# Experts' stage with half-piece weight slots, split tokens and outputs, and low parts shared between VectorE and GpSimd

## The chip, the cores and the metric

The kernel runs on one core of a Trainium2 chip, as one program for a whole stack of layers. The metric is the device time of one execution in microseconds (us); a measurement is the median of several executions.

## What is computed

A block of 256 tokens of width 1024 goes through an even layer, an odd layer with experts, and two further layers. The part that matters here is the experts' stage of the odd layer:

```python
def swiglu(h, w_gate, w_up, w_down):
    return (jax.nn.silu(h @ w_gate) * (h @ w_up)) @ w_down

def moe_swiglu(h, router, w_gate, w_up, w_down):     # h: rms_norm(x, g)
    logits = (t @ router).astype(jnp.float32)        # t: 256 x 1024
    top_v, top_i = lax.top_k(logits, TOP_K)          # 2 of 8
    top_w = jax.nn.softmax(top_v, axis=-1)
    gates = jnp.sum(jax.nn.one_hot(top_i, N_EXPERTS) * top_w[..., None], axis=1)
    for e in range(N_EXPERTS):                       # w_gate[e]: 1024 x 3584, w_down[e]: 3584 x 1024
        out = out + gates[:, e:e + 1] * swiglu(t, w_gate[e], w_up[e], w_down[e])
```

All arrays are float32. The weights of the eight experts are 352 MB, which are read once.

## The kernel before

**Split products.** Every large product is made of three products in fp32r: high by high, low by high, high by low (`split_product`, lines 174 to 176). The high part of a weight piece is a rounding copy on ScalarE (L1671 for the experts, L586 for the FFNs), the low part is raw minus high on VectorE (L1792, L593). A piece has 2048 columns in 128 partitions (1 MB).

**Steps and chunks.** The stage goes through steps `q`, one for each expert, and eight more if an expert has more than 128 tokens. A step has seven chunks of 512 hidden columns. A chunk needs six pieces: two of gate, two of up, two of down. TensorE's order in a chunk is: gate (24 products with 512 moving columns, bank 0), turn of the hidden values of the chunk before (L1591, four transposes), up (24, bank 1), down of the chunk before (24, banks 3 and 4). ScalarE makes silu (L1683), VectorE the product of silu and up (L1798), and the high and low parts of the turned hidden values (L1803, L1805).

**Between steps.** The tokens of the next expert are gathered by products of `xn` with a one-hot matrix (L1567, in f32). ScalarE and VectorE make their high and low parts with the norm's gain (L1659, L1783). The expert's output `y` is copied by both (L1711, L1835), brought back to the token order by products with the transposed one-hot matrix that carries the gate's weight (L1617, f32, the transposes are L1628), and added to the residual on VectorE (L1840). The loop runs in this order on TensorE: up of chunk 0, transposes, chunks 1 to 6, last turn, gather for the next step, last down, first half of the next gate 0, bringing back, second half. It does so in the last step too, for a step whose one-hot matrix is empty.

**Buffers.** Raw weights lie in four slots of 2 MB: slot 0 gate, slot 1 up, slots 2 and 3 down in turn. SP loads a slot again when the low parts of both its halves are made (`r_lo`). The high and low parts have three places each; a place is free when TensorE has used the piece three before (`r_used`, `PE_AHEAD`). The same four slots hold the blocks of the mixers (`load_block`); the blocks 16 to 19 wait for `r_end`, which TensorE raises when the stage is over. SP issues in the order: the FFN's pieces 0 (gate, up, down), these four blocks, the FFN's pieces 1. The mixers' and FFNs' functions are outside the experts' part of the diff. GpSimd has no work in the experts' stage.

The engines wait for semaphores only; there is no planner, the order of each engine is written out by hand.

Of the kernel before, what the change touches and what calls it, by code (L numbers as in the profile page):

```python
# [1411 lines left out]
STEPS = 2 * NE + 1  # L1412


PAIRS = 3 * NC
PE_AHEAD = 3


def moe_pair(kind, c):


    def place_of(c):
        if kind == "down":
            return PAIRS - 1 if isinstance(c, int) and c == NC - 1 else 3 * c + 4
        if isinstance(c, int) and c == 0:
            return 0 if kind == "gate" else 1
        return 3 * c - 1 if kind == "gate" else 3 * c

    first = 2 * place_of(c if isinstance(c, int) else 1) % 3
    return place_of(c), (first, (first + 1) % 3)  # L1430


def moe_done(q, kind, c):

    return 2 * (q * PAIRS + moe_pair(kind, c)[0]) + 2 + PE_AHEAD
# [31 lines left out]
def moe_load(sp, m):  # L1467
# [5 lines left out]
    def free(q, pair):  # L1473

        sp.wait_ge(s["r_lo"], 2 * (q * PAIRS + pair) + 2)

    def gate(e, c):
        sp.dma_start(r.wg, wg[bass.ds(e, 1), :, :, bass.ds(c * FC, FC)].rearrange("e p k f -> p (e k) f")).then_inc(s["r_gin"], 16)

    def up(e, c):  # L1480
        sp.dma_start(r.wu, wu[bass.ds(e, 1), :, :, bass.ds(c * FC, FC)].rearrange("e p k f -> p (e k) f")).then_inc(s["r_uin"], 16)
# [11 lines left out]
    def later(q, e, c, slot):  # L1493
        gate_up(q, e, c)
        free(q, 3 * (c - 2) + 4)
        down(e, c, slot)
# [810 lines left out]
```

## Time and profile before

| | us |
|---|---|
| median of 3 runs | 2805.64 |
| lowest and highest | 2803.16, 2812.22 |
| profiled execution, its own time | 2811.21 |
| span of its profile | 2809.0 |
| experts' stage, from the first L1628 to r_end | 706 to 1748 |

The span runs from the first to the last instruction of the core. Times in the views are counted from the span's start. A record of a matmul is longer than the distance to the next one, because matmuls are pipelined; the pace is the distance between the starts. A matmul in f32 has two records. "PEclk" is the granted clock of TensorE as a share of full speed (2.4 GHz).

### The profile page before, as it was taken

The page shows a single profiled execution, that of the slowest core. Times are in us where ns is not written, and L with a number is a line of the kernel's source. Part 1 is how long each engine was busy: PE and PEld are TensorE (multiplying, and loading weights), DVE is VectorE, ACT ScalarE, POOL GpSimd, SP SyncE. Part 2 cuts the span into 40 slices and gives each one's busy share as a digit, 9 for nine tenths or more (in the row PEclk, how much of TensorE's full clock was granted, in tenths as well). Part 3 has the DMA queues.
Part 4 walks back from the last instruction along what each step waited for, and adds up shares of the span by engine and source line. Part 5 has one row for each costly group of instructions (what it writes and reads, how often), then busy time and mean ns, then how long its engine had stood idle before and what let it go on. Part 6 is the DMA issues. An engine that isn't in the chain of part 4 may idle for free.

```text
span 2809.0 us, 36049 instructions
## 1 busy us (share of the span) xinstructions
PE 2583.0 (92%) x14026; PEld 2188.3 (78%) x14026; DVE 1768.8 (63%) x1738; ACT 1258.9 (45%) x1092; POOL 59.6 (2%) x35
## 2 busy tenths in 40 slices
PE   8699997677999999999999999899889999996999
PEld 6499884664778787878787877799659989974898
DVE  4455444443888898989898887455635555555545
ACT  2433301222666676767666766333033343321333
POOL 0000001210000000000000000000100000001000
PEclk9899998887999999999999999999889999998999
DMA  8265142002989898989899999753405575522453
GB/s 311 93 199 179 60 150 90 1 1 90 342 316 358 309 370 299 372 305 375 299 342 336 347 336 332 248 188 105 150 31 186 192 258 179 182 88 75 154 190 127
DMA packets 313325, 601.41 MB, mean 214 GB/s; under 512 B 6064, under 2 KB 130096, under 8 KB 313008
## 3 DMA queue, kind: packets, MB, share of 16 engines
q1 hardware_dynamic: 313264, 600.55, 60.4%
q8 instruction: 43, 0.70, 0.1%
q14 instruction: 18, 0.15, 0.0%
HBM read 599.48 MB, written 1.05 MB: 214 GB/s over the span
## 4 chain that ended last, share of the span: by engine, by line
PE 66%; DVE 7%; DVEq 2%; DMA 2%; ACT 2%; issue 1%; PEld 1%; PEldq 0%; ACTq 0%; SPq 0%
PE bank L174 19%; PE bank L175 18%; PE bank L176 18%; PE bank L445 3%; PE bank L1887 2%; DVE weights_lo L1792 2%; DVE scratch L2026 2%; PE bank L1567 1%; DVEq L2027 1%; PE bank L1591 1%; PE bank L1617 1%; DMA mslot<-in_o_moe_w_up 1%; DMA scratch<-in_ffn_w_gate 1%; DVEq L1778 0%; PE bank L1117 0%
## 5 line engine op out<-in xcount | busy, mean ns | idle before, releaser
L1792 DVE TENSOR_TENSOR weights_lo<-mslot,weights_hi 128x2048 fp32r<-128x2048 f32 x338 | 769.7, 2289 | 86.8 <-ACT weights_hi L1671 82.0
L1671 ACT ACTIVATE weights_hi<-mslot 128x2048 fp32r<-128x2048 f32 x338 | 646.0, 1917 | 254.1 <-PE bank L176 189.1
L593 DVE TENSOR_TENSOR weights_lo<-scratch,weights_hi 128x2048 fp32r<-128x2048 f32 x165 | 377.1, 2292 | 374.8 <-ACT weights_hi L586 372.0
L174 PE MATMUL bank<-x_hi,weights_hi 128*128 128x256 f32 x1760 | 504.4, 287 | 19.3 <-DVE weights_lo L593 10.3
L175 PE MATMUL bank<-x_lo,weights_hi 128*128 128x256 f32 x1760 | 503.6, 286 | 0.0
L176 PE MATMUL bank<-x_hi,weights_lo 128*128 128x256 f32 x1760 | 503.3, 286 | 0.0
L586 ACT ACTIVATE weights_hi<-scratch 128x2048 fp32r<-128x2048 f32 x165 | 315.6, 1919 | 323.0 <-PE bank L176 276.6
L174 PE MATMUL bank<-weights_hi,x_hi 128*128 128x512 f32 x944 | 385.6, 408 | 33.3 <-DVE weights_lo L1792 33.3
L175 PE MATMUL bank<-weights_lo,x_hi 128*128 128x512 f32 x944 | 374.3, 396 | 0.0
L176 PE MATMUL bank<-weights_hi,x_lo 128*128 128x512 f32 x944 | 374.2, 396 | 0.0
L174 PEld LDWEIGHTS bank<-x_hi,weights_hi 128*128 128x128 f32 x1760 | 343.6, 195 | 22.6 <-DVE weights_lo L593 17.6
L175 PEld LDWEIGHTS bank<-x_lo,weights_hi 128*128 128x128 f32 x1760 | 343.7, 195 | 1.7
L176 PEld LDWEIGHTS bank<-x_hi,weights_lo 128*128 128x128 f32 x1760 | 343.5, 195 | 0.0
L174 PE MATMUL bank<-weights_hi,hidden_hi 128*128 128x512 f32 x848 | 331.3, 391 | 0.0
L175 PE MATMUL bank<-weights_lo,hidden_hi 128*128 128x512 f32 x848 | 330.5, 390 | 0.0
L176 PE MATMUL bank<-weights_hi,hidden_lo 128*128 128x512 f32 x848 | 330.0, 389 | 0.0
L174 PEld LDWEIGHTS bank<-weights_hi,x_hi 128*128 128x128 f32 x944 | 181.1, 192 | 80.8 <-DVE weights_lo L1792 36.4
L176 PEld LDWEIGHTS bank<-weights_hi,x_lo 128*128 128x128 f32 x944 | 181.0, 192 | 39.9
L175 PEld LDWEIGHTS bank<-weights_lo,x_hi 128*128 128x128 f32 x944 | 181.4, 192 | 38.0 <-issue 1.9
L176 PEld LDWEIGHTS bank<-weights_hi,hidden_lo 128*128 128x128 f32 x848 | 159.2, 188 | 33.6
L174 PEld LDWEIGHTS bank<-weights_hi,hidden_hi 128*128 128x128 f32 x848 | 159.4, 188 | 31.6 <-DVE weights_lo L1792 0.2
L175 PEld LDWEIGHTS bank<-weights_lo,hidden_hi 128*128 128x128 f32 x848 | 159.4, 188 | 30.9
(346 smaller groups left out, 2312.9 us busy)
## 6 DMA issues: line engine op xcount, KB each, us to landing
mslot<-in_o_moe_w_down SPq DMA_DIRECT2D x58, 2048.0 KB, 8.1
mslot<-in_o_moe_w_gate SPq DMA_DIRECT2D x57, 2048.0 KB, 8.5
...
```

The lines of the kernel that those rows point to most:

```text
L174: pe.matmul(out, stationary[0], moving[0], start=start, stop=False)
L175: pe.matmul(out, stationary[0], moving[1], start=False, stop=False)
L176: return pe.matmul(out, stationary[1], moving[0], start=False, stop=stop)
L445: last = pe.matmul(m.ps[4 + 2 * t + half][:, :], yT[:, k, t * P:(t + 1) * P], mblock(m, i + half)[:, k, :], start=(k == 0), stop=(k == KT ...
L586: act.activation(m.whi[ffn_place(kind, u)][:, :], m.fslot[i], ACT.Copy).then_inc(m.sig["f_hi"], 1)
L593: dve.tensor_tensor(m.wlo[to][:, :], m.fslot[i], m.whi[to][:, :], ALU.subtract).then_inc(m.sig["f_lo"], 1)
L1567: last = pe.matmul(m.ps[k // 4][:, (k % 4) * P:(k % 4 + 1) * P], m.xn[:, t, k * P:(k + 1) * P], r.oh[:, t, :], start=(t == 0), stop=(t == ...
L1591: last = pe.transpose(m.ps[2][:, j * P:(j + 1) * P], r.h[:, j * P:(j + 1) * P], c["ident"])
L1671: act.activation(m.whi[places[half]][:, :], raw[:, half * PIECE:(half + 1) * PIECE], ACT.Copy).then_inc(s["r_hi"], 1)
L1792: dve.tensor_tensor(m.wlo[places[half]][:, :], raw[:, half * PIECE:(half + 1) * PIECE], m.whi[places[half]][:, :], ALU.subtract).then_inc( ...
L1887: last = pe.matmul(m.ps[bank + a // 2][:, (a % 2) * SEQ:(a % 2 + 1) * SEQ], mblock(m, base + j)[:, k, a * P:(a + 1) * P], m.xT[:, k, :], s ...
L2026: eng.scalar_tensor_tensor(c.acc[:, a, :], x, w[:, a, i:i + 1], c.acc[:, a, :], ALU.mult, ALU.add)
```

## The change

- The raw weights lie in six slots of 1 MB (three memories of 2 MB). Each half of a piece is loaded, waited for and freed by itself; a slot is loaded again when both low parts of its last content, VectorE's and GpSimd's, are made (`r_lo`, `r_lp`). The fourth memory lies over xn's high part and other tensors and isn't used in the stage.
- The pieces follow TensorE's order strictly: gate 0, up 0, gate 1, up 1, down 0, gate 2 and so on. Gate 1 of a step is loaded with gate 0 and up 0.
- VectorE makes columns 0 to 1535 of each low part, GpSimd columns 1536 to 2047 (`moe_pool`). TensorE waits for both.
- The tokens are split once: GpSimd multiplies `xn` by the gain, ScalarE makes `xnh`, GpSimd `xnl`. The gather is 16 products of each with the one-hot matrix in fp32r, and ScalarE copies the two results to `xgh` and `xgl`.
- The output is split: `yh` on ScalarE, `yl` on VectorE; bringing back is eight fp32r products with a one-hot matrix without weights, and the gate's weight is applied in the addition.
- The turned hidden values' high part goes from VectorE to ScalarE. VectorE makes the hidden product of a chunk behind the next chunk's gate low parts.
- Bringing back is in two halves, before and after up of chunk 0, and the one-hot transposes follow chunk 1.
- The last step is written out: no gather, no gate of a further step, no loads for one. The first FFN's pieces gate 0 and up 0 are split within the stage.

The diff, added lines of its core (what they replace is printed above):

```diff
-    m.mslot = [sb(f"mslot{i}", KT * HALF) for i in range(4)]
+    m.mslot = [sb(f"mslot{i}", KT * HALF) for i in range(3)]
     m.res = cut(sb("res", NT * D), 0, NT, D)
-    m.xn = cut(sb("xn", NT * D), 0, NT, D)
-    m.xT = cut(sb("xT", KT * SEQ), 0, KT, SEQ)
...
+    with nc.sbuf_tensor("mslot3", [P, KT * HALF], F32) as mslot3, nc.sbuf_tensor("xn", [P, NT * D], F32) as xn, \
+            nc.sbuf_tensor("xT", [P, KT * SEQ], F32) as xT:
+        m.mslot.append(mslot3)
+        m.xn, m.xT = cut(xn, 0, NT, D), cut(xT, 0, KT, SEQ)
+    sb("mslot3_rest", KT * HALF - NT * D)
+    m.xnh, m.xnl = cut(sb("xn_hi", NT * D, F32R), 0, NT, D), cut(sb("xn_lo", NT * D, F32R), 0, NT, D)
+    sb("xT_rest", KT * SEQ - 2 * SEQ)
+    m.oh, m.ohT = sb("one_hot", SEQ, F32R)[:, :], sb("one_hot_T", SEQ, F32R)[:, :]
...
+PIECES = 6 * NC
+PLACES, SLOTS = 3, 6
+PE_AHEAD = PLACES
+POOL_FROM = 1536
+def moe_piece(kind, c):
+    if kind == "gate":
+        return (0, 0, 0, 0) if isinstance(c, int) and c == 0 else (6 * c - 2, 1, 4, c - 1)
+    if kind == "up":
+        return (2, 2, 2, 0) if isinstance(c, int) and c == 0 else (6 * c, 0, 0, c)
+    return (40, 1, 4, 6) if isinstance(c, int) and c == NC - 1 else (6 * c + 8, 2, 2, c + 1)
+def moe_used(q, kind, c):
+    return q * PIECES + moe_piece(kind, c)[0] + 2 + PE_AHEAD
...
+    r.yh, r.yl = (flat(t)[:, KT * P:KT * SEQ] for t in (m.xh, m.xl))
+    xT = flat(m.xT)
+    r.silu, r.h = xT[:, 0:FC], xT[:, FC:2 * FC]
+    r.oh = m.oh.rearrange("p (t s) -> p t s", t=NT)
+    r.oh32, r.ohT = r.oh.bitcast(F32), m.ohT
     r.hh, r.hl = (t[:, :].rearrange("p (j t) -> p j t", j=FC // P) for t in (m.hh, m.hl))
-    r.wg, r.wu = (m.mslot[i].rearrange("p (k n) -> p k n", k=KT) for i in range(2))
-    r.wd = [m.mslot[2 + i].rearrange("p (k n) -> p k n", k=FC // P) for i in range(2)]
+    r.slot = [m.mslot[i // 2][:, i % 2 * PIECE:(i % 2 + 1) * PIECE] for i in range(SLOTS)]
+    r.gain = m.fslot[0][:, 0:D]
...
+    def piece(q, e, kind, c, begin=False):
+        number, _, slot, _ = moe_piece(kind, c)
+        n = D if kind == "down" else FC
+        raw = [half_of(kind, e, c, half) for half in range(2)]
+        if not begin:
+            for part in raw:
+                sp.lower_val(part.offset * 4)
+        for half in range(2):
+            if begin:
+                block_used(sp, m, B_SECOND - 4 + (slot + half) // 2)
+            else:
+                sp.wait_ge(s["r_lo"], q * PIECES + number + half - SLOTS + 1)
+                sp.wait_ge(s["r_lp"], q * PIECES + number + half - SLOTS + 1)
+            sp.dma_start(r.slot[slot + half].rearrange("p (k n) -> p k n", n=n),
+                         raw[half]).then_inc(s[f"r_in{slot + half}"], 16)
     def rest(q, e):
+        piece(q, e, "up", 1)
+        piece(q, e, "down", 0)
+        with sp.Fori(2, NC) as c:
+            piece(q, e, "gate", c)
+            piece(q, e, "up", c)
+            piece(q, e, "down", c - 1)
+        piece(q, e, "down", NC - 1)
+    def first(q, e, begin=False):
+        piece(q, e, "gate", 0, begin)
+        piece(q, e, "up", 0, begin)
+        piece(q, e, "gate", 1, begin)
+    sp.wait_ge(s["d_ota"], 2)
+    sp.wait_ge(s["d_otd"], 2)
+    sp.dma_start(r.gain, w["ln_ffn"][1:2, :].to_broadcast([P, D])).then_inc(s["r_gain"], 16)
+    first(0, 0, begin=True)
+    final = moe_last(sp, m)
+    with sp.Fori(0, final) as q:
+        e, after = sp.snap(q & (NE - 1), min_val=0, max_val=NE - 1), sp.snap((q + 1) & (NE - 1), min_val=0, max_val=NE - 1)
+        rest(q, e)
+        first(q + 1, after)
+    rest(final, NE - 1)
...
     def gather(n):
         pe.wait_ge(s["r_oh"], n + 1)
-                last = pe.matmul(m.ps[k // 4][:, (k % 4) * P:(k % 4 + 1) * P], m.xn[:, t, k * P:(k + 1) * P],
+        for src, banks in ((r.xnh, (5, 6)), (r.xnl, (7, 1))):
+            for k in range(KT):
+                for t in range(NT):
+                    last = pe.matmul(m.ps[banks[k // 4]][:, (k % 4) * P:(k % 4 + 1) * P],
+                                     src[:, t, k * P:(k + 1) * P], r.oh[:, t, :], start=(t == 0), stop=(t == NT - 1))
+            last.then_inc(s["r_gath"], 1)
...
+    def halves(q, kind, ch, k):
+        number, place, _, _ = moe_piece(kind, ch)
+        for half in range(2):
+            pe.wait_ge(s["r_lo"], q * PIECES + number + half + 1)
+            pe.wait_ge(s["r_lp"], q * PIECES + number + half + 1)
+            i = (place + half) % PLACES
+            yield half, [t[i][:, :].rearrange("p (k n) -> p k n", k=k) for t in (m.whi, m.wlo)]
...
     def chunk(q, ch, first=False):
         pe.wait_ge(s["r_silu"], q * NC + ch)
         inner(q, 0, "gate", ch)
+        if first:
+            pe.wait_ge(s["r_add"], q + 1)
         turn(q * NC + ch - 1)
         inner(q, 1, "up", ch)
         down(q, ch - 1, first=first)
+    def begin(q):
+        pe.wait_ge(s["r_xg"], 2 * q + 2)
+        inner(q, 0, "gate", 0)
+    def bring_back(q, t):
+        if t == 0:
+            pe.wait_ge(s["r_ohT"], q + 1)
+            pe.wait_ge(s["r_yl"], 2 * q + 2)
+        for half in range(2):
+            bank, cols = m.ps[((5, 6), (7, 2))[t][half]], slice(half * HALF, (half + 1) * HALF)
+            pe.matmul(bank[:, :], r.ohT[:, t * P:(t + 1) * P], r.yh[:, cols], start=True, stop=False)
+            pe.matmul(bank[:, :], r.ohT[:, t * P:(t + 1) * P], r.yl[:, cols], start=False,
+                      stop=True).then_inc(s["r_scat"], 1)
+    def middle(q, gather_next):
+        chunk(q, 1, first=True)
         for t in range(NT):
+            last = pe.transpose(m.ps[7][:, t * P:(t + 1) * P], r.oh32[:, t, :], c["ident"])
+        last.then_inc(s["r_ohTp"], 1)
         with pe.Fori(2, NC) as ch:
             chunk(q, ch)
         pe.wait_ge(s["r_silu"], q * NC + NC)
         turn(q * NC + NC - 1)
+        if gather_next:
+            pe.wait_ge(s["r_ohT"], q + 1)
+            gather(q + 1)
         down(q, NC - 1, final=True)
+    pe.wait_ge(s["r_xnh"], 1)
+    pe.wait_ge(s["r_xnl"], 1)
+    gather(0)
+    begin(0)
+    inner(0, 1, "up", 0)
+    final = moe_last(pe, m)
+    with pe.Fori(0, final) as q:
+        middle(q, True)
+        begin(q + 1)
+        bring_back(q, 0)
+        inner(q + 1, 1, "up", 0)
+        bring_back(q, 1)
+    middle(final, False)
+    bring_back(final, 0)
+    bring_back(final, 1)
...
+    def hi(q, kind, c, halves=(0, 1)):
+        number, place, slot, filled = moe_piece(kind, c)
+        for half in halves:
+            act.wait_ge(s[f"r_in{slot + half}"], (q * NC + filled + 1) * 16)
+            act.wait_ge(s["r_used"], q * PIECES + number + half + 1)
+            act.activation(m.whi[(place + half) % PLACES][:, :], r.slot[slot + half], ACT.Copy).then_inc(s["r_hi"], 1)
+    def gathered(n):
+        for i, (out, banks) in enumerate(((r.xgh, (5, 6)), (r.xgl, (7, 1)))):
+            act.wait_ge(s["r_gath"], 2 * n + i + 1)
+            for g in range(2):
+                last = act.activation(out[:, 4 * g:4 * g + 4, :], heads4(m.ps[banks[g]]), ACT.Copy)
+            last.then_inc(s["r_xg"], 1)
...
+    def chunk(q, c):
+        hi(q, "gate", c)
+        hi(q, "up", c)
+        hi(q, "down", c - 1, halves=(0,))
+        hidden_hi(q * NC + c - 1)
+        silu(q, c)
+        hi(q, "down", c - 1, halves=(1,))
+    def y_hi(q):
+        act.wait_ge(s["r_used"], moe_used(q, "down", NC - 1))
+        for side in range(2):
+            act.activation(r.yh[:, side * HALF:(side + 1) * HALF], m.ps[3 + side][:, :],
+                           ACT.Copy).then_inc(s["r_yh"], 1)
...
+    hi(0, "gate", 0)
+    act.wait_ge(s["r_xn"], 1)
+    act.activation(r.xnh, m.xn, ACT.Copy).then_inc(s["r_xnh"], 1)
     act.wait_ge(s["r_e"], 1)
     act.activation(r.ex, r.ex, ACT.Exp).then_inc(s["r_ed"], 1)
-        hi(q, "gate", c, m.mslot[0], "r_gin", q * NC + c + 1, halves)
-        hi(q, "up", c, m.mslot[1], "r_uin", q * NC + c + 1)
-        hi(q, "down", c - 1, m.mslot[2 + slot], f"r_din{slot}", chunks)
+    hi(0, "up", 0, halves=(0,))
...
+        middle(q)
+        hi(q + 1, "gate", 0, halves=(0,))
         gathered(q + 1)
+        hi(q + 1, "gate", 0, halves=(1,))
+        y_hi(q)
+        hi(q + 1, "up", 0)
+        silu(q + 1, 0)
+    middle(final)
+    act.wait_ge(s["r_used"], moe_used(final, "down", NC - 2))
+    ffn_hi(act, m, 1, "gate", 0)
+    y_hi(final)
+    ffn_hi(act, m, 1, "up", 0)
...
+def moe_pool(pool, m):
+    s, r = m.sig, moe_mem(m)
+    pool.wait_ge(s["r_gain"], 16)
+    pool.wait_ge(s["n_tr"], 4 * 3 + 4)
+    pool.tensor_tensor(m.xn, m.xn, bc(r.gain, 1, NT), ALU.mult).then_inc(s["r_xn"], 1)
+    pool.wait_ge(s["r_xnh"], 1)
+    pool.tensor_tensor(r.xnl, m.xn, r.xnh, ALU.subtract).then_inc(s["r_xnl"], 1)
+    def lo(q, kind, ch):
+        number, place, slot, _ = moe_piece(kind, ch)
+        for half in range(2):
+            pool.wait_ge(s["r_hi"], q * PIECES + number + half + 1)
+            i, cols = (place + half) % PLACES, slice(POOL_FROM, PIECE)
+            pool.tensor_tensor(m.wlo[i][:, cols], r.slot[slot + half][:, cols], m.whi[i][:, cols],
+                               ALU.subtract).then_inc(s["r_lp"], 1)
+    def rest(q):
+        with pool.Fori(1, NC) as ch:
+            lo(q, "gate", ch)
+            lo(q, "up", ch)
+            lo(q, "down", ch - 1)
+        lo(q, "down", NC - 1)
+    lo(0, "gate", 0)
+    lo(0, "up", 0)
+    final = moe_last(pool, m)
+    with pool.Fori(0, final) as q:
+        rest(q)
+        lo(q + 1, "gate", 0)
+        lo(q + 1, "up", 0)
+    rest(final)
...
+    def lo(q, kind, ch, halves=(0, 1)):
+        number, place, slot, _ = moe_piece(kind, ch)
+        for half in halves:
+            dve.wait_ge(s["r_hi"], q * PIECES + number + half + 1)
+            i, cols = (place + half) % PLACES, slice(0, POOL_FROM)
+            dve.tensor_tensor(m.wlo[i][:, cols], r.slot[slot + half][:, cols], m.whi[i][:, cols],
+                              ALU.subtract).then_inc(s["r_lo"], 1)
...
+    def chunk(q, ch, last=False):
+        hidden(q, ch - 1)
+        lo(q, "up", ch)
+        lo(q, "down", ch - 1, halves=(0,))
+        hidden_lo(q * NC + ch - 1)
+        lo(q, "down", ch - 1, halves=(1,))
+        if not last:
+            lo(q, "gate", ch + 1)
+    def y_lo(q):
+        for side in range(2):
+            cols = slice(side * HALF, (side + 1) * HALF)
+            dve.wait_ge(s["r_yh"], 2 * q + side + 1)
+            dve.tensor_tensor(r.yl[:, cols], m.ps[3 + side][:, :], r.yh[:, cols], ALU.subtract).then_inc(s["r_yl"], 1)
+    def add(q, t, half):
+        dve.wait_ge(s["r_scat"], 4 * q + 2 * t + half + 1)
+        x = m.res[:, t, half * HALF:(half + 1) * HALF]
+        return dve.scalar_tensor_tensor(x, m.ps[((5, 6), (7, 2))[t][half]][:, :], r.gates[:, t, bass.ds(q, 1)], x,
+                                        ALU.mult, ALU.add)
...
+    with dve.Fori(0, final) as q:
+        middle(q, True)
+        lo(q + 1, "gate", 0)
+        y_lo(q)
+        lo(q + 1, "up", 0)
+        add(q, 0, 0)
+        add(q, 0, 1)
+        lo(q + 1, "gate", 1)
+        add(q, 1, 1)
+        add(q, 1, 0).then_inc(s["r_add"], 1)
+    middle(final, False)
+    ffn_lo(dve, m, 1, "gate", 0)
+    y_lo(final)
+    add(final, 0, 0)
+    add(final, 0, 1).then_inc(s["n_res"], 1)
+    add(final, 1, 0).then_inc(s["n_res"], 1)
+    add(final, 1, 1).then_inc(s["n_res"], 1)
+    norm_scale(dve, m, AFTER_EXPERTS, 0)
+    ffn_lo(dve, m, 1, "up", 0)
...
```

## Rows read from the trace of the kernel before

**Rows 1.** Windows: span, busy (count) of PE, PEld, DVE, ACT, POOL, PEclk, DMA share, GB/s.
```profile
733.00:817.00 84.00, 84.00 (x397) 69.89 (x396) 77.62 (x50) 59.26 (x41) 0.00 (x0) 1.00 0.96 352
...
835.32:967.23 131.91, 128.61 (x575) 104.53 (x574) 114.40 (x80) 89.17 (x62) 0.00 (x0) 0.97 0.91 334
967.23:1098.01 130.78, 127.48 (x576) 103.60 (x575) 114.37 (x80) 90.98 (x62) 0.00 (x0) 0.99 0.92 337
...
1623.94:1729.80 105.86, 102.11 (x459) 83.40 (x458) 96.58 (x61) 72.17 (x43) 0.00 (x0) 1.00 0.96 350
```

**Rows 2.** Chain that ended last, 700 to 1000 us: start, us, what.
```profile
782.90 0.44 PE bank L1591 x4
...
799.71 0.44 PE bank L1591 x4
...
811.52 3.57 PE bank L1567 x32
...
823.28 3.45 PE bank L1617 x8
...
839.36 0.43 PE bank L175
```

**Rows 3.** Timeline of TensorE behind a step's border; idle time before in brackets.
```profile
838.56 0.80 PE L174 MATMUL bank<-weights_hi,x_hi 128*128 128x512 f32 x1 [2.86 <-DVE weights_lo L1792]
```

**Rows 4.** Timeline of ScalarE and VectorE at the same border.
```profile
829.49 0.60 ACT L1683 ACTIVATE xT<-bank 128x512 f32<-128x512 f32 x1 [1.96 <-PE bank L176]
832.74 3.71 ACT L1671 ACTIVATE weights_hi<-mslot 128x2048 fp32r<-128x2048 f32 x2 [2.65 <-DMA mslot<-in_o_moe_w_gate]
...
835.62 0.69 DVE L1798 TENSOR_TENSOR xT<-xT,bank 128x512 f32<-128x512 f32 x1 [3.77 <-PE bank L176]
```

**Rows 5.** Tail: ScalarE's and TensorE's timeline, and a window of saturated DMA.
```profile
1748.40 1.28 ACT L360 ACT_TABLE_LOAD   x1 [8.32 <-PEq L1645]
...
1777.99 3.71 ACT L586 ACTIVATE weights_hi<-scratch 128x2048 fp32r<-128x2048 f32 x2 [11.13 <-DMA scratch<-in_ffn_w_gate]
...
1782.28 0.58 PE L174 MATMUL bank<-x_hi,weights_hi 128*128 128x256 f32 x1 [10.29 <-DVE weights_lo L593]
...
1747.00:1777.00 30.00, 18.18 (x118) 16.82 (x116) 9.20 (x14) 13.56 (x23) 0.00 (x0) 0.88 1.06 373
```

**Rows 6.** Groups and single lines: duration by shape on VectorE and GpSimd.
```profile
L1792 DVE TENSOR_TENSOR weights_lo<-mslot,weights_hi 128x2048 fp32r<-128x2048 f32 x338 | 769.7, 2289 | 86.8 <-ACT weights_hi L1671 82.0
...
L1396 DVE TENSOR_TENSOR xn<-xn,small x2: 1209/1214/1218, 590.0 to 623.8; 128x1024 f32<-128x1024 f32 x2
...
L1178 POOL TENSOR_TENSOR scratch<-scratch,consts x12: 2342/2354/3323, 474.3 to 587.7; 128x1024 f32<-128x1024 f32 x12
...
L2070 POOL TENSOR_TENSOR scratch<-scratch 128x768 f32<-128x768 f32 x4 | 7.2, 1799 | 0.6
```

**Rows 7.** Timeline of VectorE and GpSimd, 472 to 482 us, another stage.
```profile
475.99 1.72 DVE L1353 TENSOR_TENSOR scratch<-scratch,consts 128x1024 f32<-128x1024 f32 x1
477.78 3.20 DVE L1355 TENSOR_TENSOR scratch<-consts,scratch 128x1024 f32<-128x1024 f32 x1
...
474.28 5.63 POOL L1178 TENSOR_TENSOR scratch<-scratch,consts 128x1024 f32<-128x1024 f32 x2 [7.83 <-DVE scratch L1348]
```

**Rows 8.** Timeline of TensorE in an FFN: 256 moving columns, fp32r.
```profile
1829.82 0.28 PE L174 MATMUL bank<-x_hi,weights_hi 128*128 128x256 f32 x1
1829.94 0.28 PE L175 MATMUL bank<-x_lo,weights_hi 128*128 128x256 f32 x1
```

**Rows 9.** Timeline of TensorE from the first gather to chunk 1 of step 0.
```profile
680.82 5.40 PE L1567 MATMUL bank<-scratch,xn 128*128 128x128 f32 x32 [3.45 <-DVEq L1778]
...
692.70 0.77 PE L174 MATMUL bank<-weights_hi,x_hi 128*128 128x512 f32 x1 [6.48 <-DVE weights_lo L1792]
...
709.31 0.50 PE L174 MATMUL bank<-weights_hi,x_hi 128*128 128x512 f32 x1 [2.86 <-DVE weights_lo L1792]
```

More of the change, by code:

```diff
@@ L1402, in odd_norm_dve @@
     dve.tensor_tensor(x, x, bc(o.v["orr"][:, th], 2, P), ALU.mult).then_inc(s["d_on"], 1)
[L1412 to L1435, printed above, removed]
+STEPS = 2 * NE
+PIECES = 6 * NC
[10 more added lines that the diff above has]
+    return q * PIECES + moe_piece(kind, c)[0] + 2 + PE_AHEAD
 def moe_mem(m):
@@ L1471, in moe_load @@
     wd = w["o_moe_w_down"][0].rearrange("e (k p) n -> e p k n", p=P)
[L1473 to L1481, printed above, removed]
-    def down(e, c, slot):
-        sp.dma_start(r.wd[slot], wd[bass.ds(e, 1), :, bass.ds(c * (FC // P), FC // P), :]
-                     .rearrange("e p k n -> p (e k) n")).then_inc(s[f"r_din{slot}"], 16)
@@ L1487, in gate_up @@
-    def gate_up(q, e, c):
-        free(q, 3 * (c - 1) - 1 if not isinstance(c, int) or c > 1 else 0)
-        gate(e, c)
-        free(q, 3 * (c - 1) if not isinstance(c, int) or c > 1 else 1)
-        up(e, c)
[L1493 to L1496, printed above, removed]
-    def rest(q, e):
-        gate_up(q, e, 1)
-        with sp.Fori(1, 3) as j:
-            later(q, e, 2 * j, 0)
-            later(q, e, 2 * j + 1, 1)
-        later(q, e, NC - 1, 0)
@@ L1594, in down @@
     def down(q, ch, first=False, final=False):
[L1595 to L1596 removed]
+        pe.wait_ge(s["r_hl"], q * NC + ch + 1)
+        for half, (hi, lo) in halves(q, "down", ch, FC // P // 2):
             for j in range(FC // P // 2):
@@ new lines, in y_hi, with middle @@
+    def y_hi(q):
[3 more added lines that the diff above has]
+                           ACT.Copy).then_inc(s["r_yh"], 1)
+    def middle(q):
+        chunk(q, 1)
+        act.wait_ge(s["r_ohTp"], q + 1)
+        act.activation(r.ohT, m.ps[7][:, 0:SEQ], ACT.Copy).then_inc(s["r_ohT"], 1)
+        with act.Fori(2, NC) as c:
+            chunk(q, c)
+        hi(q, "down", NC - 1)
+        hidden_hi(q * NC + NC - 1)
@@ L1732, in first_best, with one_hot, hidden, hidden_lo @@
         dve.drain()
+    def lo(q, kind, ch, halves=(0, 1)):
[5 more added lines that the diff above has]
+                              ALU.subtract).then_inc(s["r_lo"], 1)
+    def one_hot(n):
+        for t in range(NT):
+            dve.tensor_scalar(r.oh[:, t, :], c["iota"], r.rank[:, t, bass.ds(n, 1)], None, ALU.is_equal)
+        dve.drain().then_inc(s["r_oh"], 1)
+    def hidden(q, ch):
+        dve.wait_ge(s["r_used"], moe_used(q, "up", ch))
+        dve.wait_ge(s["r_silu"], q * NC + ch + 1)
+        dve.tensor_tensor(r.h, r.silu, m.ps[1][:, :], ALU.mult).then_inc(s["r_h"], 1)
+    def hidden_lo(i):
+        dve.wait_ge(s["r_hh"], i + 1)
+        dve.tensor_tensor(r.hl, heads4(m.ps[2]), r.hh, ALU.subtract).then_inc(s["r_hl"], 1)
+    def chunk(q, ch, last=False):
[16 more added lines that the diff above has]
+                                        ALU.mult, ALU.add)
+    def middle(q, more):
+        chunk(q, 1)
+        chunk(q, 2)
+        if more:
+            dve.wait_ge(s["r_ohTp"], q + 1)
+            one_hot(q + 1)
+        with dve.Fori(3, NC - 1) as ch:
+            chunk(q, ch)
+        chunk(q, NC - 1, last=True)
+        hidden(q, NC - 1)
+        lo(q, "down", NC - 1)
+        hidden_lo(q * NC + NC - 1)
     first_best(r.lg, r.m1, r.sel1)
```

251 lines of the change are left out of this document (51 added, 200 removed).

## The prediction

> **What bounds the kernel now.** I read the windows of whole expert steps first, then the chain and the timeline inside one chunk and at one step's border, then the tail. The page's busy shares are averages over stages; what counts is what ends last in the experts' stage. It has eight steps, one per expert (no overflow round). I measure a step from one pair of L1628 transposes to the next: 131.91 and 130.78 us alternate, mean 131.35 [rows 1]. From the first gate product of chunk 1 in step 0 (709.31) to the last turn of the hidden values (1729.80) it takes 1020.5 us [rows 1, 9].
>
> Inside a step TensorE paces the chunks: from turn to turn 799.71 - 782.90 = 16.81 us; less 0.44 for the turn that is 0.227 for each of 72 products, with no wait between [rows 2]. VectorE follows closely, 77.6 of 84 us busy, and DMA has a share of 0.96 at 352 GB/s [rows 1].
>
> Outside its seven chunks (117.6) a step costs 13.7 us: gather L1567 3.57, bringing back L1617 3.45 [rows 2], the two transposes some 0.25, and 6.4 more. Of this 2.9 are a hole before gate piece 1 of chunk 1 [rows 3], and most of the rest is clock: behind the hole, up to which TensorE had run nearly without a gap, the products come every 0.43 us instead of 0.227, half of full speed, so 1.2 GHz, for about 3 us of loss in one step and 1 in the next (granted clock 0.97 and 0.99 over the step) [rows 1, 2]. The hole has an order behind it: ScalarE has made that piece's high part (from 832.74, 1.9 us), but VectorE has the hidden product of chunk 0 first, which waits for the up products until 835.62; then come 0.69 of its own and 2.29 for the low part [rows 4].
>
> **Tail.** After the last turn the kernel gathers and multiplies for a ninth step that nothing uses: gather 3.6, down 5.45, half a gate 2.7, bringing back 3.45, the other half 2.7; r_end comes at 1748.40. SP loads 8 MB for it as well. Then come FFN loads (3.1 MB), four mixer blocks (6.8 MB) and only then FFN gate piece 1, copied at 1777.99; TensorE, idle for 10.3 us, restarts at 1782.28 [rows 5]. DMA is saturated there, 373 GB/s over 30 us [rows 5]: the ceiling I use.
>
> **The change, part by part.**
>
> *Steady chunk.* The 72 products and the turn stay: 16.8. What must hold is the loop of a piece: products of piece n-3 done, high part, low part, products of piece n. TensorE gives it two pieces, 5.45 us. The high part takes 1.9 [rows 4]; for the hand-over from TensorE I allow 0.2, for the others 0.05 each.
>
> The low part is now 1536 columns on VectorE and 512 on GpSimd, both released by the high part. VectorE takes 2.289 us for 2048 columns and 1.214 for 1024: 1.05 ns a column, 1.75 us for 1536, 1.60 without the start. GpSimd takes 1.80 for 768 and 2.354 for 1024: 2.16 ns a column, 1.25 us for 512, 1.11 without the start [rows 6]. Do they overlap? One place of the trace answers. GpSimd starts two L1178 at 474.28; VectorE's L1353 and L1355, with two SBUF inputs each, start at 475.99 and 477.78 and take 1.72 and 3.20 where the same size takes 1.21 alone [rows 6, 7]. Laid out with 2.34 for GpSimd's first: it ends at 476.62, VectorE's at 477.71 (1.09 later), GpSimd's second at 479.91 (2.20 later), VectorE's at 480.98 (1.07 later). They take turns by whole instructions, only the starts are hidden. So a low part lasts 1.60 + 1.11 = 2.71 and 0.15 for the start, against 2.29 now: GpSimd's help makes it later by 0.5. Six take 16.3 of a chunk's 16.8. The loop is 0.2 + 1.92 + 0.05 + 2.86 + 0.05 = 5.1 against 5.45, so the chunk stays at 16.8 with 0.35 in hand. The hidden product and hidden_lo (0.69 each) read one operand from PSUM; I take it that GpSimd goes ahead beside them. Bounds of a piece on this port: 2.25 (VectorE as now; no gain, TensorE sets 2.80) and 1.75 + 1.25 = 3.0. ScalarE takes hidden_hi (0.60) over and has 12.7 of 16.8.
>
> The Trainium skill states this for the shared port (SBUF — State Buffer, Who interferes with whom): a VectorE instruction with two SBUF inputs and a GpSimd one that reads SBUF exclude each other for their whole length. By that rule, the trace agrees with 1.72 and 3.20 against 1.21. Were the two side by side instead, a piece would be ready after 1.75 and the loop would have 1.4 in hand: the same sum, and rival D would fall away.
>
> *DMA.* Six slots of 1 MB instead of four of 2 MB; SP now waits for both engines' low parts. A slot is free when its low parts are made and needed six pieces later, less the three in the works: 12 us, room for four pieces on the way. A step's 44.04 MB at 373 GB/s are 118 us, less than the step below: hidden, as are SP's 42 issues. Without that cover each 0.1 us a piece costs 4 us a step.
>
> *Gather.* 32 fp32r products of 128 columns instead of 16 in f32, whose two records make 0.223 us each. No row has fp32r at 128 columns. Lower bound: 0.12 at 256 columns [rows 8] and 0.227 at 512 give 0.42 ns a column and 0.013, so 0.067 each, 2.1 in all. Between: a record as now, 0.11, 3.6. Upper: 0.223 each, 7.1. Nearest in shape is L1567 itself; I take 7.1 and keep 2.1 for the range. ScalarE's four copies lie beside the down products.
>
> *Border.* Bringing back is 8 fp32r products, 1.8 instead of 3.45. Gate piece 1 lies in its slots before the step and is split ahead of the hidden product, so the hole goes, and with it the low clock. y is copied (two of 0.60) and y_lo made (two of 0.69) beside gate 0. The tightest is the first up half: high part from +1.3 to +3.2 after down's end, low part to +6.05; TensorE wants it at 5.45 + 0.9 = 6.35. If a piece slips there, 1 to 2 us a step come back.
>
> New step: 117.6 + 0.25 + 7.1 + 1.8 = 126.8. The last, from gate 1 to its last turn, is 0.25 + 6 x 16.81 = 101.1. Together 7 x 126.8 + 101.1 = 988.7 against 1020.5: 31.8 less.
>
> *Start.* GpSimd multiplies xn by the gain (2048 columns, about 4.4 us) while the router works. ScalarE can't split gate 0 before r_used (677.3), then copies xn_hi until 683.1; xn_lo ends at 687.7. Gather at the slow pace of the first one now (5.40 instead of 3.57) takes 8.9 and the copies 1.4: products begin at 698.0 instead of 692.70, but gate 1 waits for nothing: 708.9 against 709.31 [rows 9]. 0.4 less.
>
> *Tail.* From the last turn: 0.45, down 5.45, y_hi and y_lo 2.2, bringing back 1.8, drain: r_end at +10.2 instead of +18.6. The blocks start there, with 3.1 MB fewer ahead of gate piece 1: 8.4 us at 373 GB/s. TensorE restarts at +10.2 + (33.9 - 8.4) = +35.7 instead of +52.5: 16.8 less. The FFN pieces made early, and the norm, lie before that restart and cost nothing while gate piece 1 sets it. The shared memory of mslot3 with xn_hi is covered by the same r_end.
>
> Sum: 31.8 + 0.4 + 16.8 = 49.0. The profiled execution took 2811.2 (span 2809.0), so 2762.2. The median of the runs is 5.6 lower: 2757.
>
> **The rivals.**
>
> A, the forecast: 2757, its own range 2745 to 2775.
>
> B, the gather costs 3.6 or less. For: one record of it takes 0.11 now. Against: f32 at 128 columns costs four times the stream. 28 us less, 2729; at 2.1 us 2717.
>
> C, small waits stay at the border (the first up half) or 0.05 us a piece in the chunks: 2 to 4 us a step, 2773 to 2790.
>
> D, the other sign: the shared port becomes the bound. Place: the low parts in the chunks. If GpSimd and all of VectorE's chunk go strictly in turns, six times 3.0 and 0.69 twice make 19.4, 2.6 over TensorE. With one piece regained during the gather a step is 126.8 + 7 x 2.6 - 2.8 = 142, eight make 123 us: 2880. It eats the gain from 49/8 = 6.1 a step on: (6.1 + 2.8)/42 = 0.21 over 2.80, so from 3.01 us a piece. For: 2.71 is only 0.09 under the pace. Against: the turns above hide their starts, and the hidden products read PSUM.
>
> That the new slots do nothing, as DMA is the bound anyway, would take 44.04 MB/126.8 = 347 GB/s as ceiling; the 373 speaks against it.
>
> **How the numbers follow.** A 0.42, B 0.27, C 0.14, D 0.17 (0.05 of it within 0.3%). The range, 2714 to 2806, holds A, B, C and D's mild end, and leaves some 0.17 out. A measurement here tells about 0.3% (8 us) from no change. Faster 0.79, same 0.05, slower 0.16.
>
> **What would show it.** Steps 127 us apart; gather records 0.22 apart (B: 0.07 to 0.11); turns 16.8 apart inside a step, VectorE's 1536 columns at 1.75 or up to 2.9 behind GpSimd; no hole and no lower clock behind the border; restart 36 us after the last turn. Wrong, towards D, if turns inside a step are over 17.3 us apart and TensorE waits for low parts there.

## The result, and the profile after the change

| | before | after |
|---|---|---|
| median of 4 runs, us | 2808.30 | 2824.19 |
| lowest and highest | 2803.16, 2812.22 | 2823.81, 2824.57 |
| profiled execution, its own time | 2811.21 | 2824.29 |
| span of its profile | 2809.0 | 2822.5 |

The ratio is 1.006 (95% interval 1.0045 to 1.0075): slower by 0.6%, where 2757 was forecast. The chip's profile says where it went. First the windows, of two whole steps and of three stretches in the second, around the transposes (columns as in [rows 1]):

```profile
861.21:994.51 133.30, 126.52 (x576) 103.90 (x575) 100.91 (x64) 90.53 (x63) 105.64 (x42) 0.97 0.92 330
994.51:1127.80 133.29, 126.53 (x576) 103.90 (x575) 100.87 (x64) 90.48 (x63) 105.53 (x42) 0.97 0.92 330
...
985.00:993.00 8.00, 7.84 (x35) 6.21 (x34) 6.03 (x4) 2.75 (x3) 2.80 (x2) 1.00 1.03 373
993.00:1002.00 9.00, 3.60 (x14) 2.78 (x13) 4.71 (x3) 5.89 (x4) 4.71 (x2) 0.76 0.32 114
...
1000.20:1004.30 4.10, 4.02 (x10) 3.19 (x11) 4.10 (x3) 0.62 (x1) 4.10 (x2) 0.50 0.67 219
```

A step takes 133.3 us; it took 131.35 [rows 1], and 126.8 was forecast. From gate 1 of step 0 to the last turn it takes 1041.8 us instead of 1020.5. TensorE is busy for 3.6 of the 9 us behind 993, and behind that its granted clock is 0.50. Its timeline: two turns of the hidden values, the transposes and what follows them, and the gather.

```profile
874.65 0.60 PE L1587 MATMUL bank<-consts,xT 128*128 128x128 f32 x4
...
891.44 0.60 PE L1587 MATMUL bank<-consts,xT 128*128 128x128 f32 x4
...
994.50 0.38 PE L1629 MATMUL bank<-consts,one_hot 128*128 128x128 f32 x2
1000.28 0.77 PE L182 MATMUL bank<-weights_hi,x_hi 128*128 128x512 f32 x1 [5.40 <-POOL weights_lo L1747]
1000.84 0.63 PE L183 MATMUL bank<-weights_lo,x_hi 128*128 128x512 f32 x1
1001.27 0.63 PE L184 MATMUL bank<-weights_hi,x_lo 128*128 128x512 f32 x1
...
1088.66 1.98 PE L1563 MATMUL bank<-one_hot,xn_hi 128*128 128x128 f32 x16
1090.48 1.95 PE L1563 MATMUL bank<-one_hot,xn_lo 128*128 128x128 f32 x16
1092.27 0.44 PE L182 MATMUL bank<-weights_hi,hidden_hi 128*128 128x512 f32 x1
```

Turns inside a step stay 16.79 apart (16.81 before, [rows 2]), but for one pair in each of the seven steps with a next one: there (891.44 to 910.08 in this step) it is 18.64, with waits of 0.63 for a low part and 0.59 for hidden_lo in chunk 3. That was the prediction's sign towards rival D, and it shows in one chunk of seven. The old hole behind the border [rows 3] is gone, and so is the low clock behind it. A new one of 5.40 us stands right behind the transposes, ahead of gate of chunk 2, in all eight steps, and behind it the products come 0.43 apart, at 1.2 GHz, until 1004.3. The releaser named is GpSimd's low part, but an engine that is named last is not yet the cause. One goes back along the same stretch on ScalarE, VectorE and GpSimd:

```profile
994.91 0.38 ACT L1703 ACTIVATE one_hot_T<-bank 128x256 fp32r<-128x256 f32 x1 [6.87 <-PE bank L1629]
995.31 5.51 ACT L1668 ACTIVATE weights_hi<-mslot 128x2048 fp32r<-128x2048 f32 x3
...
997.25 4.50 DVE L1791 TENSOR_TENSOR weights_lo<-mslot,weights_hi 128x1536 fp32r<-128x1536 f32 x2 [6.22 <-ACT weights_hi L1668]
...
997.29 8.38 POOL L1747 TENSOR_TENSOR weights_lo<-mslot,weights_hi 128x512 fp32r<-128x512 f32 x3 [7.88 <-ACT weights_hi L1668]
```

ScalarE had been idle for 6.87 us, waiting for the transposes, with its copy of them (L1703). Behind the copy in its order stand the high parts of gate of chunk 2, whose raw weights had long been loaded; three of them then come in one burst. VectorE and GpSimd were idle for 6.22 and 7.88 us behind it. TensorE, which runs the transposes at the end of chunk 1, finds all three places empty: copy 0.4, high part 1.9, low part 3.0, together with the hand-overs 5.4.

The low parts of the experts over the whole stage (duration in ns: least, median, most), and the one-hot matrix on VectorE:

```profile
L1791 DVE TENSOR_TENSOR weights_lo<-mslot,weights_hi x336: 1746/1866/2860, 679.0 to 1751.7; 128x1536 fp32r<-128x1536 f32 x168
L1747 POOL TENSOR_TENSOR weights_lo<-mslot,weights_hi x336: 1263/2812/2878, 688.6 to 1751.9; 128x512 fp32r<-128x512 f32 x168
...
L1796 DVE TENSOR_SCALAR one_hot<-consts,tiny x16: 281/1324/1343, 681.4 to 1554.3; 128x128 fp32r<-128x128 f32 x16
```

At the start, answering to [rows 9], and at the end, answering to [rows 5] (TensorE, ScalarE, SP's issues, and two windows behind r_end):

```profile
688.70 3.64 PE L1563 MATMUL bank<-one_hot,xn_hi 128*128 128x128 f32 x16 [11.74 <-POOL xn_lo L1740]
...
696.93 0.79 PE L182 MATMUL bank<-weights_hi,x_hi 128*128 128x512 f32 x1 [1.17 <-ACT x_lo L1674]
...
710.51 0.47 PE L182 MATMUL bank<-weights_hi,x_hi 128*128 128x512 f32 x1 [0.62 <-POOL weights_lo L1747]
...
1752.31 0.60 PE L1587 MATMUL bank<-consts,xT 128*128 128x128 f32 x4
1754.50 0.47 PE L182 MATMUL bank<-weights_hi,hidden_hi 128*128 128x512 f32 x1 [1.59 <-DVE hidden_lo L1806]
...
1762.24 0.75 PE L1622 MATMUL bank<-x_hi,one_hot_T 128*128 128x512 f32 x1 [2.01 <-DVE x_lo L1821]
1762.78 0.63 PE L1623 MATMUL bank<-x_lo,one_hot_T 128*128 128x512 f32 x1
1763.21 0.63 PE L1622 MATMUL bank<-x_hi,one_hot_T 128*128 128x512 f32 x1
...
1794.37 0.58 PE L182 MATMUL bank<-x_hi,weights_hi 128*128 128x256 f32 x1 [8.43 <-DVE weights_lo L601]
...
1790.08 5.51 ACT L594 ACTIVATE weights_hi<-scratch 128x2048 fp32r<-128x2048 f32 x3 [9.26 <-DMA scratch<-in_ffn_w_gate]
...
1766.05 7.42 SPq L225 DMA_DIRECT2D mslot<-in_w_in  x4
...
1766.00:1772.00 6.00, 2.52 (x15) 2.28 (x16) 4.31 (x7) 3.67 (x12) 0.00 (x0) 0.76 0.84 273
1766.05:1790.08 24.03, 16.20 (x112) 15.39 (x112) 7.49 (x14) 7.83 (x20) 0.00 (x0) 0.85 1.01 348
```

From the last turn to the FFN's restart it takes 42.1 us (52.5 before). The steps eat that gain of 10.4 and more: they lose 21.3.

### The profile page after: what moved, and what is told of

It reads as the page before. It is cut to its first block, busy times and chain, and to the rows that moved or that the text cites. A ratio compares the mean times of both kernels' runs of the same rounds, so it can differ in the third digit from the quotient of the medians.

```text
span 2822.5 us, 37757 instructions
## 1 busy us (share of the span) xinstructions
PE 2568.6 (91%) x13970; PEld 2184.4 (77%) x13970; DVE 1653.0 (59%) x1592; ACT 1264.7 (45%) x1100; POOL 921.7 (33%) x373
## 4 chain that ended last, share of the span: by engine, by line
PE 37%; POOL 22%; issue 13%; DVE 4%; DVEq 1%; ACT 1%; DMA 1%; POOLq 1%; SPq 0%; PEldq 0%; ACTq 0%; PEld 0%
POOL weights_lo L1747 22%; PE bank L182 10%; PE bank L183 10%; PE bank L184 10%; PE bank L453 3%; PE bank L1945 2%; DVE scratch L2084 2%; DVEq L2085 1%; DMA scratch<-in_ffn_w_gate 1%; PE bank L1125 0%; PE bank L1124 0%; POOLq L1751 0%; PE bank L1116 0%; SPq L225 0%; PE bank L429 0%
## 5 line engine op out<-in xcount | busy, mean ns | idle before, releaser
L1747 POOL TENSOR_TENSOR weights_lo<-mslot,weights_hi 128x512 fp32r<-128x512 f32 x336 | 851.8, 2558 | 214.4 <-ACT weights_hi L1668 212.8
L1791 DVE TENSOR_TENSOR weights_lo<-mslot,weights_hi 128x1536 fp32r<-128x1536 f32 x336 | 685.7, 2051 | 271.7 <-ACT weights_hi L1668 270.6
L182 PE MATMUL bank<-weights_hi,x_hi 128*128 128x512 f32 x936 | 378.1, 404 | 49.3 <-POOL weights_lo L1747 43.8
```

The lines of the kernel that those rows point to most:

```text
L182: pe.matmul(out, stationary[0], moving[0], start=start, stop=False)
L1747: pool.tensor_tensor(m.wlo[i][:, cols], r.slot[slot + half][:, cols], m.whi[i][:, cols], ALU.subtract).then_inc(s["r_lp"], 1)
L1791: dve.tensor_tensor(m.wlo[i][:, cols], r.slot[slot + half][:, cols], m.whi[i][:, cols], ALU.subtract).then_inc(s["r_lo"], 1)
```

## The experiments

The first theory (T) was the one above: the copy's place in ScalarE's order. Its rival (P) was the shared port: the hole is released by GpSimd, and GpSimd's low parts take 2.81 us at the median. The first four kernels form a table of the two, with one alone on the kernel before. All are compared with the kernel before on the same chip; its medians there were 2808.1 (first four kernels), 2806.4 and 2806.2, so times of different series compare to some 2 us.

**Copy of the transposes one place later.** ScalarE makes the high parts of gate of chunk 2 first.

```diff
         chunk(q, 1)
+        hi(q, "gate", 2)
         act.wait_ge(s["r_ohTp"], q + 1)
         act.activation(r.ohT, m.ps[7][:, 0:SEQ], ACT.Copy).then_inc(s["r_ohT"], 1)
-        with act.Fori(2, NC) as c:
+        hi(q, "up", 2)
+        ...
+        with act.Fori(3, NC) as c:
             chunk(q, c)
```

> The changed kernel with one move in ScalarE's order: the copy of the transposed one-hot matrix stands behind the two high parts of gate in chunk 2 instead of ahead of them. Order theory (the hole of 5.4 us behind chunk 1 comes from ScalarE waiting for the transposes with three empty places behind it, and the low clock from the hole): the hole falls under 0.7 us, the granted clock of a step rises from 0.97 to over 0.99, a step goes from 133.2 to 123.5 to 125 us, the time to about 2824 - 8 x 9 = 2752 (2740 to 2765). Port theory (GpSimd's low parts are what is late): the hole moves or shrinks by under 1 us, time 2815 to 2825.

Measured: 2763.24, ratio 0.9837 (0.982 to 0.9853): 61.0 below the changed kernel, 7.6 for each of eight steps. A step, and the two waits of TensorE over 0.3 us that are left in each step, both in chunk 3 (here of the next step):

```profile
853.66:979.28 125.62, 124.30 (x575) 102.37 (x574) 101.03 (x65) 90.64 (x63) 103.96 (x43) 1.00 0.97 351
...
1002.98 0.50 PE L182 MATMUL bank<-weights_hi,x_hi 128*128 128x512 f32 x1 [0.54 <-DVE weights_lo L1797]
1009.37 0.47 PE L182 MATMUL bank<-weights_hi,hidden_hi 128*128 128x512 f32 x1 [0.60 <-DVE hidden_lo L1812]
```

The hole is gone and the granted clock stays at 1.00. Theory T holds for the hole. The time lies in its range (2740 to 2765), the step (125.6) just above its own (123.5 to 125): something is left. One place in one engine's order decides between slower and faster than before.

**All low parts on VectorE** (`POOL_FROM = PIECE`, `moe_pool` without its low parts, no waits for `r_lp`), first on the changed kernel, then with the copy later.

> The changed kernel with all 2048 columns of each low part on VectorE; GpSimd only multiplies by the gain and makes xn_lo. Order theory: the hole behind chunk 1 shrinks only by the low part's difference (2.8 to 2.3), from 5.4 to 4.9 us, a step is 131 to 133 us, time 2805 to 2822. Port theory: the hole goes, step 124, time about 2750.

> Both edits: the copy behind gate of chunk 2, and all low parts on VectorE. Order theory: about as the first kernel, as low parts are hidden in either: 2745 to 2760; faster than the first by up to 5 us if the waits of 0.6 in chunk 2 come from the port. Were VectorE (2.25 x 6 + 2 x 0.69 = 14.9 of 16.8 a chunk) too busy at the border, slower than the first by up to 8 us.

Measured: 2800.04, ratio 0.997 (0.9958 to 0.9983), for the first, with a hole of 4.72 in every step; that is 5 us below theory T's range, and far from the 2750 of theory P. And 2745.57, ratio 0.9777 (0.976 to 0.9794), for both. A step of it:

```profile
848.09:971.33 123.24, 123.24 (x576) 102.59 (x575) 108.05 (x65) 90.71 (x63) 0.00 (x0) 1.00 0.98 357
```

TensorE is busy for 123.24 of 123.24 us: 117.6 for the chunks, 3.57 for the gather, 1.82 for bringing back, 0.25 for the transposes. The kernel is 17.7 faster than with the copy alone, where at most 5 were expected. So the hole doesn't need GpSimd (the last low part ahead of it only takes 2.29 instead of 2.81), and GpSimd's quarter costs 2.4 us a step that theory T doesn't hold. Where the hole stands, it costs more: 24.2 us between the changed kernel and the first of these two, and the copy is then worth 54.5. The two don't simply add: the shorter low part also shortens the hole, 4.72 instead of 5.40.

**GpSimd's quarter alone, on the kernel before** (`lo` on VectorE up to column 1536, the rest on GpSimd, TensorE and SP wait for both).

> The kernel before with one part of the change alone: GpSimd makes columns 1536 to 2047 of each low part. Each low part then lasts 2.8 instead of 2.3 us. Order theory (the port costs little): the hole before gate 1 grows by 0.5 us, a step by 0.5 to 1.5: 2810 to 2820. Port theory: chunks go from 16.8 to 17.5 or more, time over 2840.

Measured: 2814.64, ratio 1.0021 (1.0012 to 1.0031); steps of 129.9 to 133.7, mean 131.7, about as expected. It is 0.2% slower: in the old order too the help doesn't help.

**Half of each low part on GpSimd** (copy later, `POOL_FROM = 1024`): do the engines take turns, or does GpSimd slow down beside VectorE?

> The first kernel of the first series (copy behind gate of chunk 2) with GpSimd's share of each low part doubled: columns 1024 to 2047. Turns theory (VectorE and GpSimd exclude each other on the shared port): a piece takes 1.07 + 2.2 = 3.27 us of it, over TensorE's 2.80, so a chunk takes 19.4 to 19.8 instead of 16.8 and the time is 2763 + 8 x 13 to 8 x 17 = 2867 to 2900. If they ran side by side, GpSimd's 2.35 would stay hidden and the time would be 2755 to 2765.

Measured: 2908.45, ratio 1.0354 (1.0328 to 1.038). Consecutive waits of TensorE in a chunk, and GpSimd's low parts:

```profile
1076.69 0.47 PE L182 MATMUL bank<-weights_hi,hidden_hi 128*128 128x512 f32 x1 [0.34 <-POOL weights_lo L1753]
1080.04 0.47 PE L182 MATMUL bank<-weights_hi,x_hi 128*128 128x512 f32 x1 [0.38 <-POOL weights_lo L1753]
1083.39 0.47 PE L182 MATMUL bank<-weights_hi,x_hi 128*128 128x512 f32 x1 [0.38 <-POOL weights_lo L1753]
...
L1753 POOL TENSOR_TENSOR weights_lo<-mslot,weights_hi x336: 2346/3383/3455, 688.1 to 1839.4; 128x1024 fp32r<-128x1024 f32 x168
```

And VectorE's and GpSimd's low parts beside each other, 20 us earlier:

```profile
1056.34 1.23 DVE L1797 TENSOR_TENSOR weights_lo<-mslot,weights_hi 128x1024 fp32r<-128x1024 f32 x1 [2.15 <-ACT weights_hi L1668]
1059.06 1.85 DVE L1797 TENSOR_TENSOR weights_lo<-mslot,weights_hi 128x1024 fp32r<-128x1024 f32 x1 [1.49 <-ACT weights_hi L1668]
...
1056.42 6.76 POOL L1753 TENSOR_TENSOR weights_lo<-mslot,weights_hi 128x1024 fp32r<-128x1024 f32 x2
```

The first of GpSimd's two ends at 1059.83 by the trace, 2.26 behind VectorE's first part (1057.57), and VectorE's second part ends 1.09 behind that (1060.92). These are turns by whole instructions; neither engine works slower beside the other (alone, 2.35 and 1.21 with their starts).

A piece every 3.35 us is the sum of both engines' parts less their starts (1.21 + 2.35 = 3.56 with them, [rows 6]; 3.27 was expected, and the time lies 8 us above the range). This is the mechanism of rival D, seen at the share at which it becomes the bound.

**An eighth on GpSimd, and no one-hot matrix for the next steps** (both with the copy later). What are the 2.4 us a step that GpSimd's quarter costs? The first kernel sets `POOL_FROM = 1792`. The second leaves out the next steps' one-hot matrices (two 128x128 compares become two single columns), so all steps use the first expert's tokens.

> The first kernel of the first series with GpSimd's share halved: columns 1792 to 2047. If VectorE and GpSimd take turns, a piece holds the port for 1.87 + 0.55 = 2.42 us instead of 2.71, and what waits for GpSimd waits 0.7 instead of 1.25: step 123.3 to 124.7, time 2746 to 2757. If the loss doesn't depend on the share: 2760 to 2764.

> The first kernel of the first series (copy behind gate of chunk 2, GpSimd's quarter kept) without the 128-column one-hot instructions of the following steps: two instructions of one column take their place, so that every step gathers the first expert's tokens again (its output isn't the reference's). Theory 1 (the 2.4 us a step that GpSimd's share still costs come from the one-hot instructions that wait for it on the port, 2.1 us longer in chunk 2): chunk 2 falls from 18.6 to 16.8 to 17.0, a step from 125.7 to 123.3 to 124, seven times, 2763 to 2746 to 2751. Theory 2 (they come from the border, where additions and low parts meet): 2759 to 2763.

Measured: 2745.74, ratio 0.9781 (0.9765 to 0.9797), and 2752.49, ratio 0.9803 (0.9786 to 0.9819). A step of the one and of the other:

```profile
850.53:973.81 123.28, 123.28 (x575) 102.53 (x574) 99.78 (x65) 90.67 (x63) 97.69 (x43) 1.00 0.98 358
```

```profile
852.43:976.74 124.31, 124.07 (x576) 102.44 (x575) 100.04 (x65) 90.66 (x63) 100.94 (x43) 1.00 0.98 354
```

With an eighth every wait is gone, as with none; its time is at the lower end of the 2746 to 2757 that were expected. The second kernel lies between the two theories (2746 to 2751 and 2759 to 2763), so each holds in part. Of the 2.4 us, the one-hot matrix makes 125.66 - 124.30 = 1.4: its two instructions take 1.32 each behind GpSimd instead of 0.28. On VectorE they stand ahead of the hidden product and the low parts of chunk 3, and there the two waits of TensorE were. The other 1.1 is in small waits that no single edit here singles out: by the products' starts 0.4 of it is again in chunk 3, and 0.4 at the border.

**The one-hot matrix made twice** (copy later).

> The first kernel of the first series with the one-hot matrix on VectorE made twice. There a step is 2.4 us longer than without GpSimd's low parts, 1.8 of it in chunk 2, where the two one-hot instructions last 2.57 us together against 0.48. One-hot theory (they wait for GpSimd's instructions on the port, and the chunk has no reserve for it): another 1.3 to 2.6 us a step, 2763 + 10 to 21 = 2773 to 2784. If the 2.4 us are the port's sum over all pieces: at most 0.5 a step more, 2763 to 2767.

Measured: 2766.55, ratio 0.985 (0.9831 to 0.9869); steps of 126.0, two of 127.5. This is the range of the port's sum (2763 to 2767) and not that of the one-hot theory (2773 to 2784). The four instructions of one step, and GpSimd's low parts beside them:

```profile
L1803 DVE TENSOR_SCALAR one_hot<-consts,tiny x4: 281/803/1330, 997.9 to 1000.8; 128x128 fp32r<-128x128 f32 x4
...
993.56 6.83 POOL L1753 TENSOR_TENSOR weights_lo<-mslot,weights_hi 128x512 fp32r<-128x512 f32 x3
```

The first two waited (1.32 and 1.33), as both of the two did before; the last two took 0.29 and 0.28. They begin at 1000.56 and 1000.76, and GpSimd's last low part had ended at 1000.39. So the matrix cost 0.56 more and not 2.6 us, and this run doesn't test what it was made for. It shows only that the compare waits where a GpSimd low part runs and doesn't where none does.

**The transposes moved behind chunk 1 on the kernel before**, with ScalarE's copy behind the down halves and the one-hot matrix behind chunk 2.

> The kernel before with one part of the change alone: the one-hot transposes and ScalarE's copy of them stand behind chunk 1 (before gate of chunk 2), and the next one-hot matrix is made behind chunk 2. Order theory: a hole of 0.4 + 1.9 + 2.3 = 4.6 us appears ahead of gate in chunk 2, with 1 to 2 us of low clock behind it: 8 x 5.5 to 8 x 6.5 over the kernel before: 2852 to 2860. Otherwise within 5 us of the kernel before.

Measured: 2870.20, ratio 1.0223 (1.0197 to 1.0248). TensorE's new hole, and ScalarE at the same place:

```profile
1010.81 0.80 PE L174 MATMUL bank<-weights_hi,x_hi 128*128 128x512 f32 x1 [4.60 <-DVE weights_lo L1792]
...
1006.25 0.38 ACT L1701 ACTIVATE scratch<-bank 128x256 f32<-128x256 f32 x1 [6.47 <-PE bank L1629]
1006.53 5.50 ACT L1671 ACTIVATE weights_hi<-mslot 128x2048 fp32r<-128x2048 f32 x3
```

The same pattern in a kernel without the rest of the change: 64 us, 8.0 a step. The old hole stays beside it (3.08), and the granted clock falls to 0.95 in some steps (0.97 before), so that the price is above the 5.5 to 6.5 a step that were expected.

**The FFN's second gate and up pieces ahead of the mixers' blocks** (copy later, all on VectorE). In the tail SP issues the four blocks first, which wait for `r_end`; the DMA engines are idle meanwhile (1 GB/s from 1671 to 1685 in the kernel with the copy later and all on VectorE).

```diff
-    between()
-    gate_up(1)
+    if v == 1:
+        gate_up(1)
+        between()
+    else:
+        between()
+        gate_up(1)
     down(1)
```

> The third kernel of the first series (copy behind gate of chunk 2, all low parts on VectorE), and SP loads the next FFN's gate and up pieces 1 ahead of the four mixer blocks that wait for the end of the stage. If the wait of 8.6 us between the FFN's up 0 and gate 1 is the queue behind those blocks: it goes, with the low clock behind it, 2745.6 - 8.6 - 1 to 3 = 2734 to 2737. If the piece's slot or DMA is the limit, or the wait moves to gate 2: 2742 to 2746.

Measured: 2734.76, ratio 0.9736 (0.9718 to 0.9755): 10.8 less than without it, the fastest of all. The restart of the FFN without and with it:

```profile
1714.26 0.58 PE L182 MATMUL bank<-x_hi,weights_hi 128*128 128x256 f32 x1 [8.59 <-DVE weights_lo L601]
```

```profile
1724.15 0.38 PE L182 MATMUL bank<-x_hi,weights_hi 128*128 128x256 f32 x1 [1.42 <-DVE weights_lo L605]
```

Without it TensorE stands from 1705.7 to 1714.3; with it, it runs on there, and its first wait in that FFN is the one at 1724.15. The DMA engines load the gate piece ahead of `r_end`, where they were idle; the up piece is issued behind it, at 1689.19, but still ahead of the four blocks.

## Why the prediction was wrong

By the profiled executions 2824.3 - 2762.2 = 62.1 us are to be explained.

| step of the prediction | forecast | measured | difference |
|---|---|---|---|
| moved transposes and ScalarE's copy (the medians with and without) | 0 | 7.6 in eight steps | +61.0 |
| GpSimd's quarter, of it 1.4 by the one-hot matrix (125.66 - 123.24) | 0 | 2.4 in seven steps | +16.9 |
| gather, seven times | 7.1 | 3.57 | -24.7 |
| start (gate 1 of step 0) | 708.9 | 710.5 | +1.6 |
| tail (last turn to restart) | 35.7 | 42.1 | +6.4 |
| sum | | | +61.2 |

The other 0.9 lies behind the restart (from there to the end of the span 1028.1 us, 1026.7 before). The first two rows stand in this order: the copy moved first, then the low parts. In the other order they are 54.5 and 24.2, with nearly the same sum.

**The step that failed is the border's.** It says that the hole goes, "and with it the low clock", and the sum of the new step (117.6 + 0.25 + 7.1 + 1.8) prices the moved transposes by TensorE's 0.25 alone; ScalarE's copy of them is in no term and in no rival. The old hole went. But a step that is moved takes its waits with it, on each engine that has a part in it: the copy L1703 waits for the transposes, ScalarE runs in order, and its next high parts feed TensorE right behind the transposes. ScalarE is meant to be up to three pieces ahead of TensorE, and a wait for TensorE's present work takes that lead to nothing. The run with the copy one place later and the one with the transposes moved in the kernel before show it from both sides: 61.0 back, 64 lost. The forecast had 0.16 on slower, nearly all of it by D's port; that the change is slower comes from another cause. Of the 7.6, 5.4 is the hole and 2.1 the half clock behind it (ten distances of 0.37 to 0.56, 4.35 us, instead of ten of 0.227).

**The gather was mis-sized, case B was right.** Sixteen fp32r products of 128 columns take 1.82 us, 0.114 each: a record as in f32, but half as many per product. I had given it 0.223 from the f32 pairs, though the row of 256 columns [rows 8] spoke for less. Case B's price of 28 counts eight gathers; only seven stand between the steps, and they give 24.7.

**The port.** The turns were right (GpSimd's part waits some 1.6 for VectorE's: 2.81 at the median, 2.86 forecast with the start), and so was the chunk of 16.8, but for chunk 3: a quarter on GpSimd didn't make the port the bound of the other chunks (D). Not seen was a third customer: the one-hot matrix has one SBUF input, and waited for GpSimd all the same, 1.32 against 0.28 (it ends 0.1 behind GpSimd's low part each time). The Trainium skill states that a `tensor_scalar` can enter a mode that takes both ports, and that whoever issues first then keeps the other out for the whole instruction (SBUF — State Buffer, Who interferes with whom). By that rule, the trace agrees with the 1.32; that the compare was in such a mode no run shows by itself. The 0.35 us in hand was enough inside a chunk, and not where one more instruction came in.

**DMA** was hidden as forecast, 357 GB/s without a wait in the versions at TensorE's pace, below the 373 of saturation.

**Start.** First products at 696.93 (698.0 forecast), then 1.6 late at gate 1 by a wait of 0.62 and the half clock of the first products.

**Tail.** r_end at +13.7 and not +10.2: the last down begins 2.19 after the turn and not 0.45, because the gather that covered hidden_hi and hidden_lo is gone from the last step (a wait of 1.59), and bringing back runs at half clock, 0.43 apart, 1.7 more than forecast. The wait for y_lo ahead of it was in the sum (2.2 forecast, idle for 2.01). From r_end to the copy of the FFN's piece it takes 24.0 and not 21.2, for two reasons that together fit the 2.8: 8.4 MB are moved until then instead of 7.9, as a part of the FFN's up piece, issued at 1777.67, comes ahead of the gate piece's end; and the DMA engines start from idle, 273 GB/s in the first 6 us instead of 373. Against before, 10.4 are saved and not 16.8.

Case C (small waits, 2 to 4 us a step) came true in its size, 2.4 a step, but mostly not in its places: 1.4 of it comes by the one-hot matrix, and some 0.4 is at the border. With the copy later, the kernel gives 2763, close to the forecast's 2757. That is luck, by errors that cancel: the gather's -24.7 and the +16.9 of the port with the tail's and the start's 8.0.
